# One decoder step on one core: reads of cache pages and retention states with the heads in the four partition groups

## What is computed

```
# retention: per sample b and head h, a state S of 128 x 256
s_new = s * gamma[h] + outer(k, v)            # 8 samples, 8 heads
y     = q @ s_new                             # 1 x 128 times 128 x 256
# stick-breaking over the cache: 2 pages of 128 keys for each sample
z = einsum('bqhd,bkhd->bhqk', q, k) * scale + bias[h]
w = exp(log_sigmoid(z) + sum of -softplus(z) over the later keys)
y = einsum('bhqk,bkhd->bqhd', w, v)
```

## Time and profile before

| what | value |
|---|---|
| median of 3 runs | 3289.89 us (3289.17 to 3290.80) |
| the profiled execution | 3290.35 us |
| its span, first to last instruction | 3288.5 us |
| PE busy | 3188.0 us, 97% |
| DVE busy | 1989.8 us, 61% |
| ACT busy | 1679.0 us, 51% |
| mean granted clock of PE | 0.990 |
| first stage (slots 0 to 287) | 18.9 to 624 us |

### The profile page before, as it was taken

One profiled execution on the slowest core, in us unless ns is written; L12 is line 12 of the kernel. 1 busy time (PEld: TensorE's weight loads), 2 busy tenths in 40 slices (PEclk: granted clock), 3 DMA queues, 4 the chain that ended last, 5 costly groups with the idle time before them and its releaser, 6 DMA issues.

```text
span 3288.5 us, 59783 instructions
## 1 busy us (share of the span) xinstructions
PE 3188.0 (97%) x24637; PEld 3007.0 (91%) x24637; DVE 1989.8 (61%) x2557; ACT 1679.0 (51%) x1778; POOL 125.1 (4%) x222
## 2 busy tenths in 40 slices
PE   7999999998999999999899999999998999999997
PEld 7989888998999999999898777778998999999997
DVE  4454433577565566666767666666676556556566
ACT  3435555545454545444555555566445455455444
POOL 1010100000000000000000111000000000000000
PEclk9999999998999999999999999999999999999998
DMA  6555555553544445545455555555443444446442
GB/s 249 181 206 186 203 180 200 206 180 112 191 166 191 167 191 199 183 164 179 156 220 184 191 192 198 189 186 184 170 189 125 191 172 185 179 178 202 177 181 90
DMA packets 94087, 598.01 MB, mean 182 GB/s; under 512 B 11072, under 2 KB 11088, under 8 KB 32752
## 3 DMA queue, kind: packets, MB, share of 16 engines
q1 hardware_dynamic: 68256, 498.17, 41.2%
q0 software_dynamic: 25680, 97.69, 8.8%
HBM read 558.66 MB, written 37.15 MB: 181 GB/s over the span
## 4 chain that ended last, share of the span: by engine, by line
PE 93%; DVE 5%; ACT 1%; issue 1%; DMA 1%; DVEq 0%; POOL 0%; ACTq 0%; POOLq 0%; SPq 0%
PE acc L625 28%; PE acc L626 27%; PE acc L627 27%; PE aux L2348 2%; PE aux L2369 1%; DVE lo L558 1%; PE aux L2199 1%; PE aux L2185 1%; PE aux L2120 1%; PE aux L2022 1%; PE aux L2338 1%; DVE x L1728 1%; DVE xl L1734 1%; PE aux L2370 0%; DVE x L1718 0%
## 5 line engine op out<-in xcount | busy, mean ns | idle before, releaser
L625 PE MATMUL acc<-xh,hi 128*128 128x264 f32 x7552 | 2194.4, 291 | 74.3 <-DVE lo L558 38.6
L626 PE MATMUL acc<-xl,hi 128*128 128x264 f32 x7552 | 2151.6, 285 | 0.0
L627 PE MATMUL acc<-xh,lo 128*128 128x264 f32 x7552 | 2143.5, 284 | 0.0
L625 PEld LDWEIGHTS acc<-xh,hi 128*128 128x128 f32 x7552 | 1427.6, 189 | 141.0 <-issue 85.1
L626 PEld LDWEIGHTS acc<-xl,hi 128*128 128x128 f32 x7552 | 1428.6, 189 | 1.6
L627 PEld LDWEIGHTS acc<-xh,lo 128*128 128x128 f32 x7552 | 1425.2, 189 | 0.0
L558 DVE TENSOR_TENSOR lo<-raw,hi 128x2048 fp32r<-128x2048 f32 x473 | 1076.8, 2287 | 406.5 <-ACT hi L548 406.4
L548 ACT ACTIVATE hi<-raw 128x2048 fp32r<-128x2048 f32 x473 | 896.7, 1907 | 544.4 <-PE acc L627 317.9
L547 ACT ACTIVATE xh<-pj 128x1056 fp32r<-128x1056 f32 x144 | 156.0, 1084 | 356.7 <-PE acc L627 283.0
L555 DVE TENSOR_TENSOR xl<-pj,xh 128x1056 fp32r<-128x1056 f32 x144 | 180.8, 1255 | 247.2 <-ACT hi L548 243.5
L1443 DVE SCALAR_TENSOR_TENSOR stage<-acc,par,stage 128x255 f32<-128x255 f32 x352 | 168.9, 480 | 24.9 <-DVE stage L1443 24.4
(11 more groups left out here) (274 smaller groups left out, 1749.2 us busy)
## 6 DMA issues: line engine op xcount, KB each, us to landing
raw<-in_w SPq DMA_DIRECT2D x473, 1024.0 KB, 4.9
x<-in_ssm POOLq DMA_DIRECT2D x32, 512.0 KB, 3.9
out_ssms<-x POOLq DMA_DIRECT2D x32, 512.0 KB, 3.8
x<-in_ret POOLq DMA_DIRECT2D x16, 512.0 KB, 4.6
out_rets<-x POOLq DMA_DIRECT2D x16, 512.0 KB, 3.6
x<-in_ck POOLq DMA_DIRECT2D x16, 512.0 KB, 3.8
x<-in_cv POOLq DMA_DIRECT2D x16, 512.0 KB, 3.8
pj<-cumd POOLq DMA_DIRECT2D x32, 256.0 KB, 5.0
```

The source lines that it names most:

```text
L625: pe.matmul(out, hi[:, s, w], xh[:, a, :], start=kc == 0 and k == 0, stop=False)
L626: pe.matmul(out, hi[:, s, w], xl[:, a, :], start=False, stop=False)
L627: m = pe.matmul(out, lo[:, r, w], xh[:, a, :], start=False, stop=kc == ph.kc - 1 and k == CK - 1)
```

## The change

Heads and samples trade places. Head k of a unit (or h modulo 4 of a page) now writes the 32-row group k of `reads`; the sample is the row within it, and the stationary operand is 128x8, a diagonal of 8x8 blocks of which sample b takes block b. DVE fills these operands once for all samples (`queries_of`, `page_queries`, `page_weights`). A unit or page is one step with all its heads, at the slot where the second half stood. All samples add into the same rows, so `reads` is cleared once at the start, and the groups of matmuls span all units or pages. The copies and turns of the retention reads cover half the columns each.

```diff
-KPAGE_AT = [190 + 2 * n for n in range(NB * NPG)]
-VPAGE_AT = [240 + 2 * n for n in range(NB * NPG)]
+KPAGE_AT = [191 + 2 * n for n in range(NB * NPG)]
+VPAGE_AT = [241 + 2 * n for n in range(NB * NPG)]
...
-            def read_unit(u, x):
-                b = u % NB
-                pe.wait_ge(R["qd_set"], u + 1)
-                pe.wait_ge(R["rs_new"], 4 * u + 2 * x + 2)
...
-                for k in range(2 * x, 2 * x + 2):
-                    m = mm(reads[32 * (b % 4):32 * (b % 4) + 32, o:o + 256], qd[u % 2][:, k, :], unit[u % 3][:, k, :],
-                           start=k == 0, stop=k == 3)
+            def read_unit(u):
+                f, b = u // NB, u % NB
+                if b == 0:
+                    pe.wait_ge(R["qd_set"], f + 1)
...
+                pe.wait_ge(R["rs_new"], 4 * u + 4)
+                for k in range(4):
+                    m = mm(reads[32 * k:32 * k + NB, 256 * f:256 * f + 256], qd[:, k, NB * b:NB * b + NB],
+                           unit[u % 3][:, k, :], start=b == 0, stop=b == NB - 1)
                 m.then_inc(R["rs_y"], 1)
...
-                for k in range(4):
-                    m = turn(att[:, k * P:k * P + P], ysr[:, k * P:k * P + P])
+                for k in range(2):
+                    m = turn(att[:, k * P:k * P + P], ysr[:, 256 * f + k * P:256 * f + k * P + P])
...
-            def page_scores(n, x):
+            def page_scores(n):
...
-                for h in range(4 * x, 4 * x + 4):
-                    m = mm(reads[32 * (b % 4):32 * (b % 4) + 32, o:o + P], zq[b % 2][:, h, :], pg[:, h, :],
-                           start=h == 0, stop=h == H - 1)
-                if x:
-                    m.then_inc(R["page_used"], 1)
+                for h in range(H):
+                    o, q = (h // 4) * 256 + (1 - k) * P, 32 * (h % 4)
+                    m = mm(reads[q:q + NB, o:o + P], zq[:, h, NB * b:NB * b + NB], pg[:, h, :],
+                           start=n == 0 and h < 4, stop=n == NB * NPG - 1 and h >= 4)
+                m.then_inc(R["page_used"], 1)
...
-                    if s == UNIT_AT[u] + 3:
-                        read_unit(u, 0)
                     if s == UNIT_AT[u] + 5:
-                        read_unit(u, 1)
+                        read_unit(u)
...
-            for n in range(2):
-                dve.memset(qd[n], 0.0).then_inc(R["qd_zero"], 1)
             for j in range(LOOK):
                 split_lo(dve, ab, Step(0), j, None)
+            dve.memset(qd, 0.0).then_inc(R["qd_zero"], 1)
+            dve.memset(reads[:, :], 0.0).then_inc(R["reads_zero"], 1)
...
-            def query_of(u):
+            def queries_of(f):
                 dve.wait_ge(R["rot_done"], 8 * (f + 1))
-                if u < 2:
-                    dve.wait_ge(R["qd_zero"], u + 1)
+                if f:
+                    dve.wait_ge(R["rs_y"], NB)
                 else:
-                    dve.wait_ge(R["rs_y"], 2 * (u - 1))
+                    dve.wait_ge(R["qd_zero"], 1)
...
-                        a(pgz, reads[:, :], ACT.Identity, bias=par_of("sbrow"), scale=SCALE).then_inc(R["pg_a"], 1)
+                        for c in range(2):
+                            o = slice(256 * c, 256 * c + 256)
+                            ins = a(pgz[:, o], reads[:, o], ACT.Identity, bias=par_of("sbrow")[:, c:c + 1], scale=SCALE)
+                        ins.then_inc(R["pg_a"], 1)
...
-                        if s == KPAGE_AT[k] + x:
-                            page_scores(k, x)
-                        if s == VPAGE_AT[k] + x:
-                            page_values(k, x)
+                    if s == KPAGE_AT[k]:
+                        page_scores(k)
+                    if s == VPAGE_AT[k]:
+                        page_values(k)
```

More of the change, by code:

```diff
@@ L288, in param_layout @@
     at = 0
-    for name, width in (("lng", 4 * KT), ("lnb", 4 * KT), ("sbias", H), ("sbrow", 1), ("fcw", DEPTH * 3 * 2 * FT),
+    for name, width in (("lng", 4 * KT), ("lnb", 4 * KT), ("sbias", H), ("sbrow", 2), ("fcw", DEPTH * 3 * 2 * FT),
                         ("fcb", DEPTH * 2 * FT), ("scw", 4 * CT), ("scb", CT), ("dskip", XST),
@@ L403, in build @@
         assert at <= KT * T
[L404 to L409, removed]
+        ysr = x_[:, 3072:3584]
+        wz = [carve(x_, 3072 + 512 * n, H, NB * NB)[0] for n in range(2)]
+        zq = wz[1]
         vstk = raw_endr[:, 0:1024]
@@ L418, in build @@
         ktm = [hi_endr[:, 512 + 512 * n:1024 + 512 * n] for n in range(2)]
-        qd = [carve(hi_end, 1536 + P * n, 4, 32)[0] for n in range(2)]
+        qd = carve(hi_end, 1536, 4, NB * NB)[0]
         upper, tend = hi_end[:, 1792:1920], hi_end[:, 1920:1920 + 2 * H].rearrange("p (h c) -> p h c", c=2)
@@ L959, in read_rows @@
             def read_rows(f):
[L961 to L964, removed]
+                act.wait_ge(R["rs_y"], NB * (f + 1))
+                if not f:
                     act.wait_ge(R["rot_done"], 16)
-                a(ysr, reads[:, :], ACT.Copy).then_inc(R["ysr_in"], 1)
+                a(ysr[:, 256 * f:256 * f + 256], reads[:, 256 * f:256 * f + 256], ACT.Copy).then_inc(R["ysr_in"], 1)
             def ret_squares(h):
@@ L1068, in _ @@
                             read_rows(f)
-                    if s == KPAGE_AT[-1] + 2:
+                    if s == KPAGE_AT[-1] + 1:
                         act.wait_ge(R["page_used"], NB * NPG)
@@ L1544, in read_back @@
                 att_ready("rt", f)
[L1545 to L1550, removed]
+                for u in range(2):
+                    src = att[:, u * P:u * P + P].rearrange("p (h b) -> p h b", b=32)[:, :, 0:NB]
+                    t = VR + 8 * f + u
+                    ins = dve.tensor_copy(pt[:, t:t + 7:2, SEQ:T], src)
                 ins.then_inc(R["att_free"], 1)
@@ L1587, in sb_arg, with page_queries, page_weights @@
                 tt(zs, zs, cap, ALU.min).then_inc(R["sb_cap"], 1)
-            def page_query(b):
-                if b < 2:
-                    dve.wait_ge(R["zq_zero"], b + 1)
-                else:
[L1594 to L1609, removed]
+            def page_queries():
+                dve.wait_ge(R["zq_zero"], 1)
+                dve.wait_ge(drained, 4 * AB_PANELS.index(("qa", 1)) + 8)
+                dve.tensor_copy(zq[:, :, 0:NB * NB:NB + 1], pt[:, QA:QA + H, SEQ:T]).then_inc(R["zq_set"], 1)
+            def page_weights(k):
+                dve.wait_ge(R["wt_in"], 1)
+                if k:
+                    dve.wait_ge(R["page_used"], NB * NPG)
+                else:
+                    dve.wait_ge(R["wz_zero"], 1)
+                for c in range(2):
+                    o = (2 * c + 1 - k) * P
+                    src = wt[:, o:o + P].rearrange("p (h b) -> p h b", b=32)[:, :, 0:NB]
+                    ins = dve.tensor_copy(wz[k][:, 4 * c:4 * c + 4, 0:NB * NB:NB + 1], src)
+                ins.then_inc(R["wz_set"], 1)
             def gated(i):
@@ L1654, in _ @@
                             key_of(u)
[L1655 to L1662, removed]
+                        if s == UNIT_AT[u] - 1 and u % NB == 0:
+                            queries_of(u // NB)
+                    if s == KPAGE_AT[0] - 3:
+                        page_queries()
+                    for k in range(NPG):
+                        if s == VPAGE_AT[k] - 5 + k:
+                            page_weights(k)
                     if s == 114:
-                        for k in range(2):
-                            dve.wait_ge(R["rot_done"], 16)
-                            dve.memset(zq[k], 0.0).then_inc(R["zq_zero"], 1)
+                        dve.wait_ge(R["rot_done"], 16)
+                        dve.memset(zq, 0.0).then_inc(R["zq_zero"], 1)
                     if s == ATT_AT["rt", 1] + 1:
[L1668 to L1671, removed]
+                        dve.wait_ge(R["att_free"], ATT["rt", 1] + 1)
+                        dve.memset(wz[0], 0.0).then_inc(R["wz_zero"], 1)
+                    if s == KPAGE_AT[-1] + 2:
                         dve.wait_ge(R["pg_a"], 1)
                         stt(pge, pgz, -1.0, pgz, ALU.mult, ALU.min).then_inc(R["pg_d"], 1)
-                    if s == KPAGE_AT[-1] + 5:
+                    if s == KPAGE_AT[-1] + 4:
                         dve.wait_ge(R["pg_a"], 3)
```

50 lines of the change are left out of this document (23 added, 27 removed).

## The result

The changed kernel takes 3217.52 us (median of 4 runs, 3216.26 to 3219.49), the kernel before 3290.35 (4 runs, 3289.17 to 3290.80). The ratio is 0.978, with a 95% interval of 0.9763 to 0.9797. The kernel is faster by 72.8 us, where 50.5 were forecast. 3217.5 lies 8.5 us under the low end of the range; it is next to the rival *four at once* (3211), which had a chance of 0.08. The profiled execution took 3219.49 us, its span 3217.7.

A forecast was written before the change was run, and what follows sets the result against it. PE, busy throughout the measured stretches of the first stage, was taken to bound the kernel. Savings of 13.9 + 36.0 + 0.4 + 0.2 = 50.5 us from 3290.35 gave 3239.9 us, range 3226 to 3279.

The forecast's parts named there:

- four at once: Rival, chance 0.08: in the first stage's reads all four column groups fill and run together; 79.3 us saved, 3211 us.
- item 2: First stage's reads of units and pages: neighbouring heads in different column groups overlap in pairs, saving 36.0 us.
- no overlap: Rival, chance 0.30: each read record waits for the stream before it whatever its columns; 14.5 us saved, 3276 us.
- Item 1: Unit and page reads: 48 steps instead of 96 half steps, each excursion from main matmuls costing 0.29 us; 13.9 us saved.
- Items 3, 4 and 5: Fewer turns of retention reads, 0.4 us; query clearing moved off the start, 0.2 us; fewer small DVE copies, 0.
- Item 6: Waits that move in the first stage, such as ring slots, score copies and page weights: all covered, 0 us.
- Item 7: Transfers in the page stretches: a page lands in 3.8 us against 11.3 us of free ring slot, 0 us.
- a drain: Rival, chance 0.07: each of 272 changes of column group costs PE 0.09 us; 10 us slower, 3300 us.
- Another wait: Rival, chance 0.05: page steps wait 0.45 us for transfer or ACT; the time lands within 0.2% of before.

The follow-up runs named there:

- the run with one group: The changed kernel, but all heads of a page or unit write the same rows 0 to 7, one group of 32 columns: 3275.58 us, ratio 0.9956.
- the half steps: The changed kernel, but each page and unit read in the two half steps of before, heads in the new column groups: 3238.64 us, ratio 0.9845.

## Why the prediction was wrong, by its own steps

The frame held: PE bounds the first stage, and what PE saves there the kernel saves. The forecast failed in **item 2**, at one sentence: "So the first record of a head may start with the second of the head before it, but the next then waits for its own." Only a record's own columns hold it up. The step of a page went to four waves, not nine, and that of a unit to two, not five; 64.8 us were to be had from the reads, not 36.0. The sentence took the order in which records start in the earlier trace rows for a rule, but there all records have the same columns, so the rows could not tell order from occupied columns. The chance of 0.08 for four at once was too small for the same reason: what stood against it was no evidence. With neither end shown by a row, four at once deserved about the chance of no overlap, and the range had to take in its 3211 us. That the time came out beside a rival that had nothing in the rows for it is no merit of the prediction.

The Trainium skill, "TensorEngine Tiling (Array Packing)", "Theoretical Speedup" and "Key Properties", gives up to four times for 32 columns, with independent tiles and a drain only when the mode changes. The trace agrees: sixteen record times became four, going from group to group costs nothing that can be seen, and the 0.3 us stand where a narrow step meets products of the full width, not where small products of the full width do. "TensorE: Matmul & The Clock Gate", "Part 3: Packing small matmuls — row/col tiling", says that matmuls start and end in program order. The run with neighbours in one group, which by strict order would have been some 30 us slower, was not; here the measurement decides.

- *Item 1, excursions:* right in size. 13.9 us were forecast; the run with one group gained 605.1 - 589.6 = 15.5 us in the stage with items 1 and 3 alone (14.3 forecast), and from the half steps an excursion is 0.31 us, not 0.29. Its reading as the price of leaving the main stream was wrong: the four turns above leave it too and pay nothing.
- *Items 3, 4 and 5:* 0.4, 0.2 and 0 are too small to be told in the time. The clearing did leave the chain in front of the first `lo`, as item 4 says, but nothing came of it: the load that the chain starts with took 8.58 us where it took 8.29 before, and the first main matmul started at 19.02 us, at 18.91 before.
- *Item 6, waits that move:* wrong: it put at 0 a wait that came. It asked what covers the page weights (4.5 us; no wait appeared) and not which other chain runs beside the pages. The norms' chain had been in the trace: before the change, the squares of the third of these heads ended at 396.49 us and PE's product came at 396.64. These are rows of DVE and PE that the prediction didn't read:

```profile
396.06 0.43 DVE L1557 TENSOR_TENSOR stage<-stage 128x264 f32<-128x264 f32 x1
```

```profile
396.64 0.68 PE L2136 MATMUL aux<-stage,cons 128*128 128x264 f32 x2
```

  396.06 + 0.43 = 396.49, so 0.15 us lie between. But that much also lies between the two where PE does wait (369.91 and 370.06 in the changed kernel, 365.84 and 365.98 with the norms further apart). So there was next to no cover, and nearly any saving on PE between the two products had to become a wait. The longer wait, 2.63 us, is even more than PE saved there, 1.39 us (390.93 to 396.64 before, 5.71 us; 4.32 now). The other 1.24 us are the chain's own: before, ACT's split `hi` was half done when PE came to the first product (it ran from 389.96 to 391.87), and now it had not begun. With the shorter wait and the clock, 4.6 us went.
- *Item 7, transfers:* right for the changed kernel, where no wait of PE ends with a landing. But the landing time was not constant: a page lands in 4.6 to 5.2 us, not 3.8, and the one issued beside the store of the cache rows took 9.3, where it took 4.3 beside the same store before the change. Two versions waited for that page (0.5 us with half steps, 1.0 with the norms further apart); with the store moved none did. Item 7 left the store out.
- *The rivals:* no overlap was measured by the run with one group, 3275.6, where 3276 stood. No price of a change of columns was seen: a page step with its seven changes took 0.75 us, where over 2.5 stood for a drain. Another wait did come, but took 4.6 of 79 us.

The sum by the mechanism that holds is 13.9 + 64.8 + 0.4 - 4.6 = 74.5 us in the stage; 73.9 were measured. 3 us longer later stages leave 70.9 for the profiled execution, 3290.35 - 3219.49.

## What to carry to other kernels

Where an operand uses few columns of the array and its stream sets the pace, put independent products into different column groups and let them stand together in one step: here four streams ran in the time of one, whatever the order of the heads, and the same was worth another 31 us in a later stage. Rows in which every neighbour shares a resource can't show whether order or the resource holds them up, so both cases need a fair chance. And before PE is made faster by several microseconds in a stretch, list every chain of the other engines in that stretch with the time between its end and PE's use of it, less the lag that is there even when PE waits (here 0.15 us); the smallest such margin shows which wait will come first.

## What the runs showed of the hardware

- Four products of plain fp32, two records each, run side by side in four groups of 32 columns: 0.75 us for a step whose records alone took 2 x 0.90 before.
- A step with operands of 32 or 8 columns between main matmuls of 128 costs about 0.3 us beside its records, by three readings: 0.29 in the earlier trace rows, 0.31 from the half steps, (15.5 - 0.4) / 48 = 0.31 from the run with one group. Four turns at the full width cost 0.44 us, their records alone.
- After PE had been idle for 2.63 us it ran at the higher level for about a microsecond more, then at the lower for 3.4 us. That a wait costs more than its length was not in the prediction's sums.
